# Norm edges between products: one-column sums and wider filler matmuls

## The chip, the core and the metric

The kernel runs on one core of one Trainium2 chip. The metric is device time in microseconds (us). The kernel before takes 2642.19 us, the median of three runs (2640.82 to 2643.86). The engines are named as in the profile: PE is TensorE, PEld its weight loads, DVE is VectorE, ACT is ScalarE, POOL is GpSimd, SP the queue that issues the DMAs. The time is that of the whole program, one launch.

## The reference

Two model blocks in f32, with 512 tokens of width 1024. The first block is a hybrid mixer of four recurrences, cross-attention to a memory, and a convolutional feed-forward network (FFN). The second has two layers whose norms are shifted and scaled by a vector computed from a condition: a layer with a gated recurrence and sparse attention, a layer with a short convolution, each with an FFN. What the change touches is the norm that stands between two matrix products of the second block:

```python
def rms_norm(x, g):
    xf = x.astype(jnp.float32)
    y = xf * lax.rsqrt(jnp.mean(xf * xf, axis=-1, keepdims=True) + EPS)
    return (y * g.astype(jnp.float32)).astype(x.dtype)

def second_block(x, c, ...):
    for i in range(DEPTH_2):
        ...
        h = rms_norm(x, norm_mix_pre[i]) * (1.0 + sc_m) + sh_m
        y = mixer(h, ...)
        x = x + (1.0 + g_m) * rms_norm(y, norm_mix_post[i])
        h = rms_norm(x, norm_ffn_pre[i]) * (1.0 + sc_f) + sh_f
        y = conv_ffn(h, ...)
        x = x + (1.0 + g_f) * rms_norm(y, norm_ffn_post[i])
    return x
```

## The kernel before

All activations lie feature-major: a tile is 128 features by 512 tokens, and 1024 features are KT = 8 tiles. A product multiplies them with weights that stream through a ring of six slots. DVE splits each weight slot into a high and a low part (L324, L326), and PE makes three passes of 128x512 for each pair of tiles (L369, L370, L371); these passes are reduced-precision f32 and one record each in the profile. A plain f32 matmul is two records, with a weight load each.

Between two products stands an edge. Its work is written out by hand, each engine's instructions in program order, with semaphores between the engines; nothing reorders them. The function edge builds four of them (ffn_norm_1, sc_norm, ffn_norm_2 and last_norm), double_edge one (ab_norm). In edge:

- ACT squares the eight output tiles of the product before, POOL adds seven of them. PE adds over the features by matmuls with a constant of ones: L479 for the sum of seven, L482 for the last square, four matmuls each, one for each 128 tokens. The tokens are the stationary operand, the ones the moving one, so every output column holds the same sum.
- ACT takes the root of column 0 (L502), DVE inverts it (L524), PE spreads the four columns over all partitions (spread_root, L471).
- DVE then makes h + y * gain * rstd for eight tiles in turn (L536, L540). For each one ACT squares it (L514) and PE adds it to a second sum (L493, four matmuls). This is the loop of eight turns.
- After the eighth turn root, inverse and spread follow again, and DVE and ACT make the eight tiles that the next product reads (L547, L519, L553). The first of them releases PE's first pass of that product. In last_norm there is no second norm: its PE work ends with the first spread, and the output is stored tile by tile.

Between these steps PE issues matmuls whose result nobody reads, into PSUM bank 1: keep_busy (L662), identity times ones, 128 columns each. There are 11 before the loop, one in each of the first seven turns, and eight behind the second spread.

double_edge joins two norms. Its PE work is L585 (hidden behind the last square), then L588, then L594 and L595 in turns for the second sum, spread_root (L576) for the first norm, three fillers, L576 for the second, eight fillers. Between the spreads stands DVE's inverse L638, which is queued behind the first L620.

Of the kernel before, what the change touches and what calls it, by code (L numbers as in the profile page):

```python
# [24 lines left out]
ALU = mybir.AluOpType  # L25
# [7 lines left out]
P = 128  # L33
# [423 lines left out]
def edge(k, name, before, first_gain, gain=None, shift=None, then=None, y=None):  # L457
# [8 lines left out]
    ones = k.const("ones")  # L466
# [9 lines left out]
    def tensor(pe):  # L476
        pe.wait_ge(added, KT - 1)
        for c in range(TT):
            nc.tensor.matmul(k.psum[:, SUMS + c, 0:P], k.sum_sq[:, c * P:(c + 1) * P], ones, start=True, stop=False)  # L479
        pe.wait_ge(squared, KT)  # L480
        for c in range(TT):
            last = nc.tensor.matmul(k.psum[:, SUMS + c, 0:P], k.squares[:, (KT - 1) % 2, c * P:(c + 1) * P],  # L482
                                    ones, start=False, stop=True)
        last.then_inc(summed, 1)
        spread_root(pe, 0)
        if gain is None:
            return
        pe.wait_ge(out, KT - 2)
        keep_busy(k, pe, 11)
        for j in range(KT):  # L490
            pe.wait_ge(resquared, j + 1)
            for c in range(TT):
                last = nc.tensor.matmul(k.psum[:, SUMS + c, P:2 * P], k.squares[:, j % 2, c * P:(c + 1) * P], ones,  # L493
                                        start=(j == 0), stop=(j == KT - 1))
            last.then_inc(counted, 1)
            if j < KT - 1:
                keep_busy(k, pe, 1)
        spread_root(pe, 1)
        keep_busy(k, pe, 8)

    def root(act, i):
        nc.scalar.activation(k.roots[:, i, :].unsqueeze(2), k.psum[:, SUMS:SUMS + TT, i * P:i * P + 1], ACT.Sqrt,  # L502
                             bias=k.const("eps"), scale=1.0 / D).then_inc(rooted, 1)
# [56 lines left out]
def double_edge(k, name, before, first_gain, gain, shift, then):  # L560
# [10 lines left out]
    ones = k.const("ones")  # L571
# [9 lines left out]
    def tensor(pe):  # L581
        last = (KT - 1) % 2
        pe.wait_ge(added, KT - 1)
        for c in range(TT):
            nc.tensor.matmul(k.psum[:, SUMS + c, 0:P], k.sum_sq[:, c * P:(c + 1) * P], ones, start=True, stop=False)  # L585
        pe.wait_ge(squared, KT)
        for c in range(TT):
            end = nc.tensor.matmul(k.psum[:, SUMS + c, 0:P], k.squares[:, last, c * P:(c + 1) * P], ones,  # L588
                                   start=False, stop=True)
        end.then_inc(summed, 1)  # L590
        pe.wait_ge(added_scaled, KT - 1)
        pe.wait_ge(squared_scaled, KT)
        for c in range(TT):
            nc.tensor.matmul(k.psum[:, SCALED, c * P:(c + 1) * P], k.rstd[:, c * P:(c + 1) * P], ones, start=True, stop=False)  # L594
            end = nc.tensor.matmul(k.psum[:, SCALED, c * P:(c + 1) * P], k.scaled_squares[:, last, c * P:(c + 1) * P], ones,  # L595
                                   start=False, stop=True)
        end.then_inc(summed, 1)
        spread_root(pe, 0)
        keep_busy(k, pe, 3)
        spread_root(pe, 1)  # L600
        keep_busy(k, pe, 8)
# [13 lines left out]
    def vector(dve):  # L615
        link = Link(dve, steps)

        def renew(j):
            if j < KT:
# [11 lines left out]
        nc.vector.tensor_tensor(k.roots[:, 1, :].unsqueeze(2), k.roots[:, 2, :].unsqueeze(2),  # L631
                                k.psum[:, SCALED, :].rearrange("p (c x) -> p c x", x=P)[:, :, 0:1], ALU.mult
# [26 lines left out]
def keep_busy(k, pe, n):  # L659

    for _ in range(n):
        k.nc.tensor.matmul(k.psum[:, 1, 0:P], k.const("ident"), k.const("ones"), start=True, stop=True)  # L662
# [2435 lines left out]
def build(nc, dram, wheres, vec_at):  # L3098

    with ExitStack() as ctx:  # L3100
# [86 lines left out]
        k.roots = k.sb("roots", [P, 4, TT])  # L3187
# [208 lines left out]
```

## Time and profile before

| | before |
|---|---|
| median of three runs | 2642.19 us |
| the profiled execution: its time | 2640.82 us |
| its span (first to last instruction) | 2639.0 us |
| PE busy / PEld busy | 2431.9 / 1974.1 us |
| DVE / ACT / POOL busy | 1751.0 / 666.2 / 207.0 us |
| mean granted clock of PE | 0.956 |
| matmuls of the edges: L493, L662, L471, L482, L479 | 192, 178, 56, 32, 32 records |

PE is busy for 92% of the span. The granted clock is a share of 2.4 GHz; the profile knows two levels, 1.00 and 0.50 (1.2 GHz), and the mean says that PE ran at half clock in some stretches. The views used below: the timeline shows instructions in order of time, merged where the same one repeats; the windows show for a stretch of time how long each engine was busy, how many instructions it had (x) and the granted clock (PEclk). A busy PE is one that has an instruction, which may be one that streams a single column.

### The profile page before, as it was taken

What the parts mean: (1) busy time and instruction counts of PE and PEld (TensorE: products, weight loads), DVE (VectorE), ACT (ScalarE), POOL (GpSimd) and SP (SyncE); (2) the same over time, 40 slices, a digit from 0 to 9 for tenths busy, and PEclk for the clock granted to TensorE, in tenths of its full rate; (3) what the DMA queues carried; (4) which work ended last, traced back from release to release, by engine and by line L of the source; (5) the groups of instructions that cost most, each with busy time, mean ns of one, the idle gap of its engine ahead of it and who ended that gap; (6) DMA issues with size and microseconds to landing.
All of it is one profiled execution on the core that took longest, in us unless ns stands there. A gap on an engine that the chain in (4) does not pass through costs nothing. (4 is left out here: it accounts for less than half of the span.)

```text
span 2639.0 us, 34212 instructions
## 1 busy us (share of the span) xinstructions
PE 2431.9 (92%) x13854; PEld 1974.1 (75%) x13854; DVE 1751.0 (66%) x2724; ACT 666.2 (25%) x1234; POOL 207.0 (8%) x177
## 2 busy tenths in 40 slices
PE   4998877779989999999897979999999999999997
PEld 3885766677678888888674558888888888888886
DVE  6674563774778886525878867766665887766654
ACT  2222332001111120221256760222210211322200
POOL 1001340100100001100013101000001001000000
PEclk9998895889999999999997989999999999999999
DMA  4220001242123335421220007133365353233342
GB/s 150 80 86 2 3 2 49 64 137 71 52 85 96 96 124 199 141 72 64 72 70 18 2 33 262 66 98 99 97 210 183 129 197 130 70 96 96 106 153 68
DMA packets 69324, 252.80 MB, mean 96 GB/s; under 512 B 7696, under 2 KB 7984, under 8 KB 68528
## 3 DMA queue, kind: packets, MB, share of 16 engines
q1 hardware_dynamic: 68592, 248.35, 28.4%
q8 instruction: 110, 1.80, 0.3%
q10 hardware_dynamic: 576, 2.28, 0.2%
q14 instruction: 46, 0.38, 0.0%
HBM read 248.50 MB, written 2.10 MB: 95 GB/s over the span
## 5 line engine op out<-in xcount | busy, mean ns | idle before, releaser
L369 PE MATMUL psum<-rounded_n,rounded_high 128*128 128x512 f32 x1856 | 738.3, 398 | 5.7 <-DVE rounded_n_low L553 2.1
L370 PE MATMUL psum<-rounded_n_low,rounded_high 128*128 128x512 f32 x1856 | 727.9, 392 | 0.0
L371 PE MATMUL psum<-rounded_n,rounded_ring 128*128 128x512 f32 x1856 | 727.2, 392 | 0.0
L326 DVE TENSOR_TENSOR rounded_ring<-ring,rounded_high 128x1024 fp32r<-128x1024 f32 (+1 forms) x360 | 444.5, 1235 | 12.4
L369 PEld LDWEIGHTS psum<-rounded_n,rounded_high 128*128 128x128 f32 x1856 | 352.3, 190 | 87.1 <-issue 11.7
L370 PEld LDWEIGHTS psum<-rounded_n_low,rounded_high 128*128 128x128 f32 x1856 | 352.2, 190 | 76.5 <-issue 4.3
L371 PEld LDWEIGHTS psum<-rounded_n,rounded_ring 128*128 128x128 f32 x1856 | 351.9, 190 | 74.5
L324 DVE CAST rounded_high<-ring 128x1024 fp32r<-128x1024 f32 (+1 forms) x360 | 246.1, 684 | 238.7 <-PE psum L371 223.3
L369 PE MATMUL psum<-rounded_arena,rounded_high 128*128 128x512 f32 x720 | 281.5, 391 | 10.6 <-DVE rounded_ring L326 10.6
L370 PE MATMUL psum<-rounded_arena,rounded_high 128*128 128x512 f32 x720 | 281.1, 390 | 0.0
L371 PE MATMUL psum<-rounded_arena,rounded_ring 128*128 128x512 f32 x720 | 281.1, 390 | 0.0
L2214 DVE SCALAR_TENSOR_TENSOR scratch<-arena,vecs,scratch 128x512 f32<-128x512 f32 x88 | 65.8, 748 | 163.0 <-ACT scratch L2201 163.0
L369 PEld LDWEIGHTS psum<-rounded_arena,rounded_high 128*128 128x128 f32 x720 | 135.8, 189 | 39.1 <-DVE rounded_ring L326 10.9
L371 PEld LDWEIGHTS psum<-rounded_arena,rounded_ring 128*128 128x128 f32 x720 | 135.8, 189 | 28.4
L370 PEld LDWEIGHTS psum<-rounded_arena,rounded_high 128*128 128x128 f32 x720 | 135.9, 189 | 28.2
L2195 ACT COPY arena<-psum 128x512 f32<-128x512 f32 x88 | 51.7, 587 | 351.3 <-PE psum L371 351.3
L2201 ACT ACTIVATE scratch<-arena,vecs 128x512 f32<-128x512 f32 x88 | 63.8, 725 | 199.6 <-DVE arena L2235 198.2
L2288 ACT ACTIVATE scratch<-psum 128x512 f32<-128x512 f32 x32 | 19.2, 600 | 321.9 <-PE psum L371 321.9
L425 POOL TENSOR_TENSOR sum_sq<-sum_sq,scratch 128x512 f32<-128x512 f32 x45 | 68.8, 1530 | 301.8 <-ACT scratch L2288 242.4
L422 POOL COPY sum_sq<-scratch 128x512 f32<-128x512 f32 x7 | 5.1, 725 | 1094.1 <-ACT scratch L2288 838.3
L798 DVE CUSTOM_DVE_ANT_0 arena<-arena 128x1024 f32<-128x1024 f32 x48 | 61.9, 1332 | 14.1 <-DMA arena<-in_mod_w 14.1
L798 DVE CUSTOM_DVE_ANT_0 n_low<-n_low 128x1024 f32<-128x1024 f32 x48 | 56.7, 1220 | 19.6 <-DMA n_low<-in_mod_w 19.6
(466 smaller groups left out, 3050.5 us busy)
## 6 DMA issues: line engine op xcount, KB each, us to landing
ring<-in_w_up SPq DMA_DIRECT2D x132, 512.0 KB, 3.4
ring<-in_w_down SPq DMA_DIRECT2D x48, 512.0 KB, 3.5
n_low<-in_mod_w SPq DMA_DIRECT2D x48, 512.0 KB, 5.2
arena<-in_mod_w SPq DMA_DIRECT2D x48, 512.0 KB, 5.4
ring<-in_w_ab_in SPq DMA_DIRECT2D x37, 512.0 KB, 3.5
ring<-in_w_mix_in SPq DMA_DIRECT2D x31, 512.0 KB, 3.5
ring<-in_w_sc_in SPq DMA_DIRECT2D x24, 512.0 KB, 4.8
ring<-in_w_down SPq DMA_DIRECT2D x24, 384.0 KB, 3.2
```

Source lines behind the costliest of these rows:

```text
L324: nc.vector.tensor_copy(self.rounded(high), raw).then_inc(self.weights_rounded, 1)
L326: nc.vector.tensor_tensor(self.rounded(raw), raw, self.rounded(high), ALU.subtract).then_inc(self.weights_split, 1)
L369: self.nc.tensor.matmul(out, w_high, x_high, start=first, stop=False)
L370: self.nc.tensor.matmul(out, w_high, x_low, start=False, stop=False)
L371: return self.nc.tensor.matmul(out, w_low, x_high, start=False, stop=last)
L422: nc.gpsimd.tensor_copy(total, sq).then_inc(added, 1)
L425: nc.gpsimd.tensor_tensor(total, total, sq, ALU.add).then_inc(added, 1)
L798: k.nc.vector.tensor_tensor_reduce(out=self.tiles[:, i % 3], in0=self.tiles[:, i % 3], in1=self.cond, scale=1.0, scalar=0.0, op0=ALU.mult, ...
L2195: nc.scalar.copy(x, k.psum[:, j % PRODUCT_BANKS, :]).then_inc(out, 1)
L2201: nc.scalar.activation(dst, x, ACT.Copy, scale=taps[:, col:col + 1]).then_inc(tapped, 1)
L2214: link(nc.vector.scalar_tensor_tensor(dst, src[:, 0:T], taps[:, col:col + 1], dst, ALU.mult, ALU.add))
L2288: nc.scalar.activation(k.squares[:, j % 2, :], k.psum[:, j % PRODUCT_BANKS, :], ACT.Square).then_inc(squared, 1)
```

## The change

The sums over features get a moving operand of one column in place of 128, so each writes one column of PSUM, and the readers (L502, L605, L631) are adapted. keep_busy's matmul gets wider, 512 moving columns in place of 128, and is called less often: in edge twice before the loop (11 before) and twice behind it (8 before), in double_edge once and twice (3 and 8 before). Inside the loop stands a filler of 256 columns after each of the eight turns, the eighth included, where there was one of 128 after the first seven. The fillers read the table of vectors instead of ones. The tile of roots has three rows in place of four, since double_edge uses three.

```diff
--- before.py
+++ after.py
@@ -463,7 +463,7 @@
         k.sem(f"{name}_{s}") for s in ("summed", "rooted", "inverted", "spread", "renewed", "resquared", "counted",
                                        "scaled", "shifted", "steps", "done"))
     SUMS, SPREAD = 4, 2
-    ones = k.const("ones")
+    one = k.const("ones")[:, 0:1]
 
     def spread_root(pe, i):
         pe.wait_ge(inverted, i + 1)
@@ -476,30 +476,29 @@
     def tensor(pe):
         pe.wait_ge(added, KT - 1)
         for c in range(TT):
-            nc.tensor.matmul(k.psum[:, SUMS + c, 0:P], k.sum_sq[:, c * P:(c + 1) * P], ones, start=True, stop=False)
+            nc.tensor.matmul(k.psum[:, SUMS + c, 0:1], k.sum_sq[:, c * P:(c + 1) * P], one, start=True, stop=False)
         pe.wait_ge(squared, KT)
         for c in range(TT):
-            last = nc.tensor.matmul(k.psum[:, SUMS + c, 0:P], k.squares[:, (KT - 1) % 2, c * P:(c + 1) * P],
-                                    ones, start=False, stop=True)
+            last = nc.tensor.matmul(k.psum[:, SUMS + c, 0:1], k.squares[:, (KT - 1) % 2, c * P:(c + 1) * P], one,
+                                    start=False, stop=True)
         last.then_inc(summed, 1)
         spread_root(pe, 0)
         if gain is None:
             return
         pe.wait_ge(out, KT - 2)
-        keep_busy(k, pe, 11)
+        keep_busy(k, pe, 2)
         for j in range(KT):
             pe.wait_ge(resquared, j + 1)
             for c in range(TT):
-                last = nc.tensor.matmul(k.psum[:, SUMS + c, P:2 * P], k.squares[:, j % 2, c * P:(c + 1) * P], ones,
+                last = nc.tensor.matmul(k.psum[:, SUMS + c, 1:2], k.squares[:, j % 2, c * P:(c + 1) * P], one,
                                         start=(j == 0), stop=(j == KT - 1))
             last.then_inc(counted, 1)
-            if j < KT - 1:
-                keep_busy(k, pe, 1)
+            nc.tensor.matmul(k.psum[:, 1, 0:T // 2], k.const("ident"), k.vecs[:, 0:T // 2], start=True, stop=True)
         spread_root(pe, 1)
-        keep_busy(k, pe, 8)
+        keep_busy(k, pe, 2)
 
     def root(act, i):
-        nc.scalar.activation(k.roots[:, i, :].unsqueeze(2), k.psum[:, SUMS:SUMS + TT, i * P:i * P + 1], ACT.Sqrt,
+        nc.scalar.activation(k.roots[:, i, :].unsqueeze(2), k.psum[:, SUMS:SUMS + TT, i:i + 1], ACT.Sqrt,
                              bias=k.const("eps"), scale=1.0 / D).then_inc(rooted, 1)
 
     def scalar(act):
@@ -568,7 +567,7 @@
                                        "steps", "done"))
     SUMS, SPREAD, SCALED = 4, 3, 0
     AHEAD = 3
-    ones = k.const("ones")
+    one = k.const("ones")[:, 0:1]
 
     def spread_root(pe, i):
         pe.wait_ge(inverted, i + 1)
@@ -582,23 +581,23 @@
         last = (KT - 1) % 2
         pe.wait_ge(added, KT - 1)
         for c in range(TT):
-            nc.tensor.matmul(k.psum[:, SUMS + c, 0:P], k.sum_sq[:, c * P:(c + 1) * P], ones, start=True, stop=False)
+            nc.tensor.matmul(k.psum[:, SUMS + c, 0:1], k.sum_sq[:, c * P:(c + 1) * P], one, start=True, stop=False)
         pe.wait_ge(squared, KT)
         for c in range(TT):
-            end = nc.tensor.matmul(k.psum[:, SUMS + c, 0:P], k.squares[:, last, c * P:(c + 1) * P], ones,
+            end = nc.tensor.matmul(k.psum[:, SUMS + c, 0:1], k.squares[:, last, c * P:(c + 1) * P], one,
                                    start=False, stop=True)
         end.then_inc(summed, 1)
         pe.wait_ge(added_scaled, KT - 1)
         pe.wait_ge(squared_scaled, KT)
         for c in range(TT):
-            nc.tensor.matmul(k.psum[:, SCALED, c * P:(c + 1) * P], k.rstd[:, c * P:(c + 1) * P], ones, start=True, stop=False)
-            end = nc.tensor.matmul(k.psum[:, SCALED, c * P:(c + 1) * P], k.scaled_squares[:, last, c * P:(c + 1) * P], ones,
+            nc.tensor.matmul(k.psum[:, SCALED, c:c + 1], k.rstd[:, c * P:(c + 1) * P], one, start=True, stop=False)
+            end = nc.tensor.matmul(k.psum[:, SCALED, c:c + 1], k.scaled_squares[:, last, c * P:(c + 1) * P], one,
                                    start=False, stop=True)
         end.then_inc(summed, 1)
         spread_root(pe, 0)
-        keep_busy(k, pe, 3)
+        keep_busy(k, pe, 1)
         spread_root(pe, 1)
-        keep_busy(k, pe, 8)
+        keep_busy(k, pe, 2)
 
     def scalar(act):
         act.wait_ge(summed, 1)
@@ -628,8 +627,7 @@
         dve.wait_ge(summed, 2)
 
         link(nc.vector.tensor_tensor(k.roots[:, 2, :], k.roots[:, 2, :], k.roots[:, 0, :], ALU.mult))
-        nc.vector.tensor_tensor(k.roots[:, 1, :].unsqueeze(2), k.roots[:, 2, :].unsqueeze(2),
-                                k.psum[:, SCALED, :].rearrange("p (c x) -> p c x", x=P)[:, :, 0:1], ALU.mult
+        nc.vector.tensor_tensor(k.roots[:, 1, :], k.roots[:, 2, :], k.psum[:, SCALED, 0:TT], ALU.mult
                                 ).then_inc(scaled, 1)
         dve.wait_ge(spread, 1)
         dve.wait_ge(out, KT)
@@ -659,7 +657,7 @@
 def keep_busy(k, pe, n):
 
     for _ in range(n):
-        k.nc.tensor.matmul(k.psum[:, 1, 0:P], k.const("ident"), k.const("ones"), start=True, stop=True)
+        k.nc.tensor.matmul(k.psum[:, 1, :], k.const("ident"), k.vecs[:, 0:T], start=True, stop=True)
 
 
 def load_inputs(k):
@@ -3184,7 +3182,7 @@
                                              k.vec("ffn_norm")))
         k.tables.pop()
         k.clear_stage_semaphores()
-        k.roots = k.sb("roots", [P, 4, TT])
+        k.roots = k.sb("roots", [P, 3, TT])
         k.arena = k.sb("arena", [P, 50 * T])
         k.rest = k.sb("rest", [P, 476])
         hidden_buffers(k)
```

PE's program at the edge ffn_norm_1, from its first sum into the loop, before (consts is the identity or ones, scratch a square; xN repeats):

```order
L479 MATMUL psum<-consts,sum_sq 128x128 x4
L482 MATMUL psum<-consts,scratch 128x128 x4
L471 MATMUL psum<-consts,roots 128x128 x4
L662 MATMUL psum<-consts 128x128 x11
L493 MATMUL psum<-consts,scratch 128x128 x4
L662 MATMUL psum<-consts 128x128
L493 MATMUL psum<-consts,scratch 128x128 x4
L662 MATMUL psum<-consts 128x128
```

and now (vecs is the table of vectors that the fillers read):

```order
L479 MATMUL psum<-consts,sum_sq 128x1 x4
L482 MATMUL psum<-consts,scratch 128x1 x4
L471 MATMUL psum<-consts,roots 128x128 x4
L660 MATMUL psum<-vecs,consts 128x512 x2
L493 MATMUL psum<-consts,scratch 128x1 x4
L496 MATMUL psum<-vecs,consts 128x256
L493 MATMUL psum<-consts,scratch 128x1 x4
L496 MATMUL psum<-vecs,consts 128x256
```

The order of the steps is the same; the eleven fillers are two wide ones, the sums have one column, and the filler of a turn has 256. The loop's end on PE, before:

```order
L493 MATMUL psum<-consts,scratch 128x128 x4
L662 MATMUL psum<-consts 128x128
L493 MATMUL psum<-consts,scratch 128x128 x4
L471 MATMUL psum<-consts,roots 128x128 x4
L662 MATMUL psum<-consts 128x128 x8
L369 MATMUL psum<-rounded_n,rounded_high 128x512
```

and now:

```order
L493 MATMUL psum<-consts,scratch 128x1 x4
L496 MATMUL psum<-vecs,consts 128x256
L493 MATMUL psum<-consts,scratch 128x1 x4
L496 MATMUL psum<-vecs,consts 128x256
L471 MATMUL psum<-consts,roots 128x128 x4
L660 MATMUL psum<-vecs,consts 128x512 x2
L369 MATMUL psum<-rounded_n,rounded_high 128x512
```

One filler has come between the last sum and the spread. The double edge on PE, from the last pair of the second sum to the last filler, before:

```order
L594 MATMUL psum<-consts,rstd 128x128
L595 MATMUL psum<-consts,scratch 128x128
L576 MATMUL psum<-consts,roots 128x128 x4
L662 MATMUL psum<-consts 128x128 x3
L576 MATMUL psum<-consts,roots 128x128 x4
L662 MATMUL psum<-consts 128x128 x8
```

and now:

```order
L593 MATMUL psum<-consts,rstd 128x1
L594 MATMUL psum<-consts,scratch 128x1
L575 MATMUL psum<-consts,roots 128x128 x4
L660 MATMUL psum<-vecs,consts 128x512
L575 MATMUL psum<-consts,roots 128x128 x4
L660 MATMUL psum<-vecs,consts 128x512 x2
```

Nothing has moved past a spread there; widths and counts alone differ. DVE's, ACT's, POOL's and SP's programs have the same instructions in the same order, with L631 reading four neighbouring columns.

## Rows read from the trace of the kernel before

**Rows 1.** The page, parts 1 and 2: busy time of PE; its granted clock in 40 slices.

```profile
PE 2431.9 (92%) x13854; PEld 1974.1 (75%) x13854; DVE 1751.0 (66%) x2724; ACT 666.2 (25%) x1234; POOL 207.0 (8%) x177
...
PEclk9998895889999999999997989999999999999999
```

**Rows 2.** The page, part 4: the chain that ended last, by line.

```profile
PE psum L369 12%; PE psum L371 12%; PE psum L370 12%; PE psum L493 1%; PE psum L662 0%; PE psum L471 0%; DVE h L540 0%; DVE n L536 0%; PE psum L482 0%; PE psum L479 0%; DVE rounded_n_low L553 0%; DVE n_low L547 0%; ACT rounded_n L519 0%; ACT roots L502 0%; DVE roots L524 0%
```

**Rows 3.** Timeline, edge ffn_norm_1: start, us, engine, line, operation, xcount, [idle before].

```profile
1666.96 0.97 PEld L482 LDWEIGHTS psum<-consts,scratch 128*128 128x128 f32 x8
...
1668.69 0.97 PEld L471 LDWEIGHTS psum<-consts,roots 128*128 128x128 f32 x8 [0.76 <-DVE roots L524]
...
1669.68 2.62 PE L662 MATMUL psum<-consts 128*128 128x128 f32 x22
1669.89 0.75 DVE L536 SCALAR_TENSOR_TENSOR n<-n,mod_cols,psum 128x512 f32<-128x512 f32 x1 [1.25 <-PE psum L471]
...
1672.07 0.97 PEld L493 LDWEIGHTS psum<-consts,scratch 128*128 128x128 f32 x8
...
1673.45 0.97 PEld L493 LDWEIGHTS psum<-consts,scratch 128*128 128x128 f32 x8 [0.19 <-ACT scratch L514]
...
1683.48 1.16 PE L471 MATMUL psum<-consts,roots 128*128 128x128 f32 x8 [0.57 <-DVE roots L524]
...
1687.08 0.19 PEld L369 LDWEIGHTS psum<-rounded_n,rounded_high 128*128 128x128 f32 x1 [0.85 <-issue]
```

**Rows 4.** Timeline, the double edge.

```profile
1097.21 0.39 PE L371 MATMUL psum<-rounded_arena,rounded_ring 128*128 128x512 f32 x1
...
1099.04 0.97 PEld L588 LDWEIGHTS psum<-consts,scratch 128*128 128x128 f32 x8 [0.74 <-ACT scratch L1983]
...
1101.72 0.97 PEld L576 LDWEIGHTS psum<-consts,roots 128*128 128x128 f32 x8
...
1103.59 0.17 DVE L638 RECIPROCAL roots<-roots 128x4 f32<-128x4 f32 x1
```

**Rows 5.** Windows, the loop of ffn_norm_1: stretch, us, busy (x), PEclk, DMA, GB/s.

```profile
1672.10:1683.40 11.30, 10.80 (x80) 9.28 (x79) 8.89 (x14) 4.67 (x8) 0.00 (x0) 1.00 0.01 1
```

**Rows 6.** Windows of L860 alone, then of L662 alone: PE and PEld.

```profile
87.90:90.20 2.30, 2.29 (x22) 2.29 (x21) 1.00 0.50 134
...
1669.80:1672.10 2.30, 2.30 (x22) 2.30 (x21) 1.00 0.01 4
```

**Rows 7.** Matmul durations of L2383 and L493: ns min/median/max.

```profile
L2383 PE MATMUL psum<-vecs,arena x64: 182/250/353, 1160.5 to 1183.1; 128*128 128x1 f32 x64
...
L493 PE MATMUL psum<-consts,scratch x192: 275/275/377, 1672.1 to 2258.0; 128*128 128x128 f32 x192
```

**Rows 8.** Timeline of PE: f32 matmuls with 256 and 512 columns.

```profile
647.28 1.89 PE L2071 MATMUL psum<-mem_k,z_att 128*128 128x256 f32 x8
...
1239.78 1.88 PE L2414 MATMUL psum<-arena 128*128 128x512 f32 x4
```

**Rows 9.** Windows around one run of L2383.

```profile
1179.50:1182.60 3.10, 3.10 (x30) 3.09 (x29) 0.00 (x0) 0.00 (x0) 0.00 (x0) 1.00 0.00 0
1182.80:1189.40 6.60, 6.60 (x18) 5.33 (x18) 0.16 (x1) 0.00 (x0) 0.00 (x0) 0.50 0.00 0
1189.60:1192.00 2.40, 2.40 (x12) 1.97 (x11) 0.00 (x0) 0.03 (x1) 0.00 (x0) 1.00 0.00 0
```

**Rows 10.** Window over L1494 (two columns) at half clock.

```profile
442.10:448.80 6.70, 6.70 (x33) 6.70 (x33) 2.12 (x3) 3.09 (x5) 0.00 (x0) 0.50 0.89 352
```

**Rows 11.** Windows at the end of the projection ab_in.

```profile
1394.00:1397.60 3.60, 1.45 (x7) 0.87 (x5) 3.53 (x4) 2.63 (x6) 0.53 (x1) 1.00 0.27 92
1397.80:1404.00 6.20, 0.00 (x0) 0.00 (x0) 6.13 (x6) 4.53 (x8) 3.77 (x3) 0.50 0.06 22
```

**Rows 12.** Timeline of PE: product matmuls at half clock.

```profile
1184.79 0.63 PE L369 MATMUL psum<-rounded_n,rounded_high 128*128 128x512 f32 x1
1185.21 0.63 PE L370 MATMUL psum<-rounded_n_low,rounded_high 128*128 128x512 f32 x1
```

## The prediction

> **What bounds the kernel now.** I read the page first. TensorE (PE) is busy 2431.9 of 2639.0 us and its granted clock is full in most slices [rows 1], and in the chain of waits the matmuls of the products stand first; of the edges' own lines only L493 reaches 1% [rows 2]. So the kernel is bound by PE nearly everywhere, and where it is not, by short chains between PE, ACT and DVE. The change touches such chains alone: the five edges, that is the norm between two products.
>
> Next, the timeline of one edge, which stands for three (ffn_norm_1, sc_norm and ffn_norm_2 run alike) [rows 3]. When ACT has the product's last square, four sums over 128 columns (L482) start their loads, at 1666.96; four spreads start at 1668.69; DVE gets them at 1669.89. Then comes a loop of eight turns. Its pace is DVE's: the loads of L493 start 1.38 us apart (1672.07, 1673.45) and PE's loads stand only 0.19 us in between. After the eighth turn PE idles 0.57 us for the root and its inverse, runs the spread from 1683.48, and the next product starts at 1687.08. PE waits there for DVE and ACT, so its fillers (L662) are free as long as they end in time. The double edge is shorter: from 1099.04 PE runs 12 sum matmuls in one piece until the spread at 1101.72, and a second spread waits for L638 [rows 4]. In all of this the granted clock is 1.00 [rows 5].
>
> **The change, term by term, with the clock as it is.** In the rows one f32 matmul is two records.
>
> Narrow sums. Is a matmul with one moving column cheaper than one with 128? In one stretch of 2.30 us at full clock 21 loads of L860 (two columns) start; in 2.30 us of L662 (128 columns) also 21 [rows 6]. Both are 0.11 us apart: the load of 128 stationary columns sets the pace, and the change keeps these loads. Only the last record ends sooner, 250 for 275 ns, and the first after a stop takes 182 for 377 ns [rows 7]; since the second record waits for the first, I take 0.1 us for a group of four, bounds 0.03 and 0.2. Eight groups are on a path (four first sums of the edges, three last turns, one in the double edge): -0.8 us. The 16 records of L594 and L595 keep their pace, so the spread at 1101.72 stays.
>
> The Trainium skill ("TensorE: Matmul & The Clock Gate", section "Back-to-back issue gap") gives about 60 cycles for 1 to 64 columns, a floor near 25 ns; by that alone eight records would take 0.2 us instead of 0.9. Its section on LDWEIGHTS gives columns over 1.2 GHz, 107 ns for 128, and with that one the trace agrees (0.11 us).
>
> Fillers. A 128x256 record takes 0.216 us (eight in 1.89, the last 0.38 long) and a 128x512 record 0.43 us (four in 1.88, the last 0.59) [rows 8]. First filler: 22 x 0.112 = 2.46 us becomes 4 x 0.43 = 1.72, ending at 1671.4, before L493's first load at 1672.07; no effect. In a turn, 8 x 0.112 + 0.43 = 1.32 us against DVE's 1.38: it just fits. The new one after the eighth turn, 0.43, lies in the 0.57 us of root and inverse. The last, 1.79 becomes 1.72, lies before 1687.08. Double edge: 0.67 becomes 0.86; from 1101.72 spread (0.89) and filler end at 1103.47, L638's result is there at 1103.77. Four columns fewer in roots and L631's read cost nothing. Sum at full clock: 2640.8 - 0.8 = 2640.0.
>
> **The clock.** What changes more is what PE streams. Before, a turn streams 128 columns in all of its ten records, back to back for 1.12 of 1.38 us. After, wide work is 0.43 us of 1.38, and 0.89 us goes to records that load 128 columns and stream one. What the clock does on such work the trace shows at L2383, also one column wide: in 1179.50 to 1182.60 PE is busy all the time with 30 such records at clock 1.00, and then the clock is 0.50 in 1182.80 to 1189.40, nearly all of it dense product already [rows 9]. L1494, two columns wide, stays at half all through 33 records with PE busy [rows 10]. And a stretch with less than half wide work loses it too: 1394.0 to 1397.6 holds 1.45 us of product, no more, and 0.50 follows [rows 11]. The loop has less wide work than that, 0.43 of 1.38 us against 1.45 of 3.60, and it lasts 11 us. So I expect the clock to fall from 2.4 to 1.2 GHz inside each of the three loops. No row fixes the turn; the dense first filler guards the first of them, and I take the fall after three of the eight.
>
> At half clock a narrow record takes 6.7 us / 33 = 0.21 us [rows 10], and a product's record 0.42 to 0.43 us (1184.79 to 1185.21) [rows 12], both about twice what they take at full clock; the filler's record of 256 columns took 0.216 at full clock and takes, doubled like these, 0.43, its two 0.85. A turn: 8 x 0.213 + 0.85 = 2.56 us. PE, not DVE, then sets the pace: 1.18 us more for each of about five turns, 5.9 us (bounds: two turns, 2.4; seven, 8.3). Behind the loop (all at half clock): filler 0.85 for a wait of 0.57, +0.3; spread 8 x 0.213 for 8 x 0.112, +0.8; last fillers 3.41 us for the 2.7 between the spread's last load and 1687.08, and then product at half clock until it rises, +1.1 together or more. But these are 5 us of dense work, and after 6.6 us of such work the clock was back in rows 9; I take half of this 2.2, 1.1, bounds 0.3 and 4. Less the 0.2 of narrow sums: 5.9 + 1.1 - 0.2 = 6.8 us an edge, 20.4 for three.
>
> Double edge: from the product's end at 1097.6 to 1101.72 PE streams next to nothing, so the clock falls in or just behind it. Full cost if it falls midway: 8 records of sums x 0.1, the spread 0.8, the filler 1.71 for the 1.2 until L638's result, 0.5; 2.1 us. Falling later costs about 0.5. I take 1.3 (bounds -0.1 and 2.7). The last edge has one spread behind its sums: 0.1, at most 0.7. Sum: 2640.8 + 20.4 + 1.3 + 0.1 = 2662.6. The profiled execution, 2640.82 with its span of 2639.0, lies 1.4 below the median 2642.19; half of this added gives 2663.
>
> **Rivals.**
> 1. The clock holds: one wide filler in each turn is enough, and no stop of PE is longer than before by much. For it: PE stays "busy" in nearly all of the loop, and the fillers are there. Then the sum at full clock stands, 2640.0 to 2642: no change. Against: rows 9, busy all the time and fallen. The Trainium skill (same page, section "Why this matters for your kernels") asks only that no long idle gaps part the matmuls; by this rule the clock would hold in the loop, and the time would be this rival's. The trace disagrees at L2383.
> 2. It falls only where hardly anything is streamed (behind the products, 1666.96 to 1668.69 and in the double edge) or in one loop, and the wide fillers bring it back: two or three falls of 1 to 3 us, or one loop of 6.8; 2643 to 2649, say 2646. For it: the first filler is dense for 1.72 us.
> 3. The other side, faster: one-column matmuls cost by their columns after all, since L860 and L2383 read other operands. Then eight groups on a path lose 0.8 us each, and the 16 records of L594 and L595 1.2 more: 2640.8 - 7.6 = 2633. It decides if eight L493 records take under 0.3 us. Against: rows 6, at the same load of 128 columns.
>
> **How the numbers follow.** Forecast (half clock in all three loops) 0.72, own range 2651 to 2672: 3.5 to 10 us for each loop. Rival 1: 0.12. Rival 2: 0.12. Rival 3: 0.04. The range starts at 2644, above rival 1 and taking in most of rival 2, and goes to 2673: it leaves out rivals 1 and 3 and a little of the rest, 0.2 in all. A change of 0.2% (5.3 us) is about what a measurement can tell from none. Slower by more: the forecast and most of rival 2, 0.81. Faster by more: rival 3, 0.04. Same: 0.15.
>
> **What would show it.** Clock 0.50 in stretches inside the loops of L493 and near 1100 us; L493's loads 2.56 us apart in these and 1.38 before the fall; eight loads of L493 in 0.9 us at full clock, not 0.2; the first load of L482 to the next product's first load some 27 us apart where it was 20.1. A granted clock of 1.00 through all loops would make the prediction wrong, and so would narrow records that are less than 0.1 us apart.

## The result and the profile after

The changed kernel takes 2677.8 us (median of 4 runs, 2676.6 to 2681.1), beside it the kernel before 2641.9 (2640.8 to 2643.9): ratio 1.0135, 95% interval 1.0118 to 1.015, slower. The prediction had the sign, but 2663 and the upper end 2673 were too low. The profiled execution, which is not one of these four, took 2672.26 us with a span of 2670.4, so 31.4 us more in the span than before.

The page after, parts 1, 2 and 4: busy time of PE, its clock in 40 slices, the chain by line.

```profile
PE 2467.2 (92%) x13754; PEld 1984.5 (74%) x13754; DVE 1747.2 (65%) x2724; ACT 666.5 (25%) x1234; POOL 210.0 (8%) x177
...
PEclk9998986899999999999897999899999899899999
...
PE psum L369 12%; PE psum L370 12%; PE psum L371 12%; PE psum L493 1%; PE psum L496 1%; PE psum L471 0%; DVE n L535 0%; DVE h L539 0%; PE psum L660 0%; DVE rounded_ring L326 0%; DVE rounded_high L324 0%; DVE rounded_n_low L552 0%; DVE n_low L546 0%; ACT rounded_n L518 0%; ACT scratch L513 0%
```

Against [rows 1, 2], the clock has an 8 in slices 26, 32 and 35 (each 66.8 us wide), the slices of the three edges with a loop, where it had a 9, and L496, the filler in the loop, has entered the chain. (Lines behind the loop's filler stand one or two numbers lower than before: L660 is the filler L662, L513 is L514, L575 is L576, L593 and L594 are L594 and L595.)

The edge ffn_norm_1 in the timeline after, answering [rows 3]: its front, the loads of the loop's turns, and its end.

```profile
1671.71 0.97 PEld L482 LDWEIGHTS psum<-consts,scratch 128*128 128x128 f32 x8
...
1673.33 0.97 PEld L471 LDWEIGHTS psum<-consts,roots 128*128 128x128 f32 x8 [0.65 <-DVE roots L523]
...
1676.71 0.97 PEld L493 LDWEIGHTS psum<-consts,scratch 128*128 128x128 f32 x8 [1.33 <-ACT scratch L513]
...
1678.09 0.97 PEld L493 LDWEIGHTS psum<-consts,scratch 128*128 128x128 f32 x8 [0.19 <-ACT scratch L513]
...
1680.86 0.97 PEld L493 LDWEIGHTS psum<-consts,scratch 128*128 128x128 f32 x8 [0.19 <-ACT scratch L513]
...
1682.27 2.04 PEld L493 LDWEIGHTS psum<-consts,scratch 128*128 128x128 f32 x8
...
1684.50 0.63 ACT L513 ACTIVATE scratch<-h 128x512 f32<-128x512 f32 x1 [0.93 <-PE psum L493]
1684.83 2.04 PEld L493 LDWEIGHTS psum<-consts,scratch 128*128 128x128 f32 x8
...
1692.65 1.91 PEld L471 LDWEIGHTS psum<-consts,roots 128*128 128x128 f32 x8 [0.23 <-DVE roots L523]
...
1697.29 0.19 PEld L369 LDWEIGHTS psum<-rounded_n,rounded_high 128*128 128x128 f32 x1 [1.16 <-issue]
```

Up to the fourth turn the loads are 1.38 us apart, with the wait of 0.19 for ACT between; from the fifth they are 2.56 apart (1682.27, 1684.83), PE no longer waits, and ACT waits for PE. The windows before and behind that point answer [rows 5]:

```profile
1672.10:1681.80 9.70, 8.63 (x57) 6.66 (x57) 8.28 (x13) 3.05 (x7) 0.00 (x0) 1.00 0.16 53
...
1681.90:1695.50 13.60, 13.60 (x53) 12.14 (x52) 4.46 (x8) 2.45 (x5) 0.00 (x0) 0.50 0.01 1
```

PE is "busy" for all of the second stretch, at 1.2 GHz. The edge sc_norm does the same, but ffn_norm_2 doesn't: there the clock falls twice, once just behind the first wide filler's start and again after the loop's third turn.

```profile
2265.60:2268.90 3.30, 3.30 (x6) 1.24 (x5) 3.19 (x5) 1.00 (x2) 0.00 (x0) 0.50 0.01 2
2269.00:2272.30 3.30, 3.30 (x27) 3.20 (x28) 3.20 (x6) 1.42 (x3) 0.00 (x0) 1.00 0.00 0
2272.40:2289.40 17.00, 17.00 (x63) 14.92 (x63) 5.86 (x10) 3.38 (x6) 0.00 (x0) 0.50 0.00 0
```

The other place where time went is one that the change doesn't name: the products that read the arena. The arena is the large tensor whose tiles are the moving operand of 2160 passes (3 x 720 records). Here are its groups at L369 and L370, of before and then of after.

```profile
L369 PE MATMUL psum<-rounded_arena,rounded_high 128*128 128x512 f32 x720 | 281.5, 391 | 10.6 <-DVE rounded_ring L326 10.6
L370 PE MATMUL psum<-rounded_arena,rounded_high 128*128 128x512 f32 x720 | 281.1, 390 | 0.0
```

```profile
L369 PE MATMUL psum<-rounded_arena,rounded_high 128*128 128x512 f32 x720 | 285.2, 396 | 10.6 <-DVE rounded_ring L326 10.6
...
L370 PE MATMUL psum<-rounded_arena,rounded_high 128*128 128x512 f32 x720 | 284.9, 396 | 0.0
```

Durations overlap, so the pace is better read from the number of loads in 100 us. Windows in the last feed-forward block at clock 1.00: the first is inside its second product (reads the arena), the other inside its first (reads n); before, then after.

```profile
2500.00:2600.00 100.00, 100.00 (x443) 82.84 (x442) 52.97 (x64) 10.32 (x17) 8.66 (x6) 1.00 0.43 138
2300.00:2400.00 100.00, 100.00 (x443) 82.84 (x442) 61.92 (x81) 23.75 (x38) 0.00 (x0) 1.00 0.31 96
```

```profile
2540.00:2640.00 100.00, 100.00 (x430) 80.36 (x429) 45.01 (x57) 7.54 (x14) 13.30 (x7) 1.00 0.35 108
2320.00:2420.00 100.00, 100.00 (x443) 82.77 (x442) 63.95 (x85) 22.64 (x37) 0.00 (x0) 1.00 0.31 98
```

With n as moving operand there are 442 loads in both kernels. With the arena there are 429 after: a pass takes 0.233 us instead of 0.226, in a window where PE never stops and the clock is full.

**The 31.4 us by place.** Taking the first load of each product and of each edge as marks, the double edge lasts 14.25 us (before 11.29), the three others 26.66, 26.70 and 28.68 (before 21.19 each) and the last 17.53 (17.64). That is 2.96 + 5.47 + 5.51 + 7.49 - 0.11 = 21.3 us. The stretches of product that read the arena got longer too: 359.97 to 363.50, 358.74 to 362.25 (twice), 173.76 to 175.03 and 89.47 to 90.64, together 13.0. The sum is 34.3; the remaining -2.9 lies in stretches that the change leaves alone (-2.5 of it in the first 737 us). Executions differ by more than that there: the double edge begins between 1093.7 and 1103.5 us in four profiled executions whose program is the same up to there (the kernel before and three of the experiments below).

### The profile page after: what moved, and what is told of

Read it like the earlier page. It is cut to its first block and busy times, and to the rows that moved or that the text cites. A ratio compares the mean times of both kernels' runs of the same rounds, so it can differ in the third digit from the quotient of the medians.

```text
span 2670.4 us, 34012 instructions
## 1 busy us (share of the span) xinstructions
PE 2467.2 (92%) x13754; PEld 1984.5 (74%) x13754; DVE 1747.2 (65%) x2724; ACT 666.5 (25%) x1234; POOL 210.0 (8%) x177
## 5 line engine op out<-in xcount | busy, mean ns | idle before, releaser
L369 PE MATMUL psum<-rounded_n,rounded_high 128*128 128x512 f32 x1856 | 738.8, 398 | 4.1 <-DVE rounded_n_low L650 1.9
L370 PE MATMUL psum<-rounded_n_low,rounded_high 128*128 128x512 f32 x1856 | 728.3, 392 | 0.0
L326 DVE TENSOR_TENSOR rounded_ring<-ring,rounded_high 128x1024 fp32r<-128x1024 f32 (+1 forms) x360 | 442.0, 1228 | 12.4
L369 PEld LDWEIGHTS psum<-rounded_n,rounded_high 128*128 128x128 f32 x1856 | 352.9, 190 | 88.5 <-issue 12.9
L370 PEld LDWEIGHTS psum<-rounded_n_low,rounded_high 128*128 128x128 f32 x1856 | 352.7, 190 | 76.9 <-issue 4.3
L369 PE MATMUL psum<-rounded_arena,rounded_high 128*128 128x512 f32 x720 | 285.2, 396 | 10.6 <-DVE rounded_ring L326 10.6
L370 PE MATMUL psum<-rounded_arena,rounded_high 128*128 128x512 f32 x720 | 284.9, 396 | 0.0
L369 PEld LDWEIGHTS psum<-rounded_arena,rounded_high 128*128 128x128 f32 x720 | 135.3, 188 | 43.8 <-DVE rounded_ring L326 10.9
L370 PEld LDWEIGHTS psum<-rounded_arena,rounded_high 128*128 128x128 f32 x720 | 135.4, 188 | 33.1
L796 DVE CUSTOM_DVE_ANT_0 arena<-arena 128x1024 f32<-128x1024 f32 x48 | 61.9, 1333 | 14.3 <-DMA arena<-in_mod_w 14.3
```

Of the source, the lines that this page charges most:

```text
L326: nc.vector.tensor_tensor(self.rounded(raw), raw, self.rounded(high), ALU.subtract).then_inc(self.weights_split, 1)
L369: self.nc.tensor.matmul(out, w_high, x_high, start=first, stop=False)
L370: self.nc.tensor.matmul(out, w_high, x_low, start=False, stop=False)
L796: k.nc.vector.tensor_tensor_reduce(out=self.tiles[:, i % 3], in0=self.tiles[:, i % 3], in1=self.cond, scale=1.0, scalar=0.0, op0=ALU.mult, ...
```

## The experiments

The theory for the first batch: two causes, the arena's place (13 to 14 us) and the clock lost to the narrow sums in the loops (about 21). Rivals: the arena's products are slow for another reason, a late effect of the edges; and the clock falls for the thinner fillers, not the sums.

**The changed kernel with four rows in roots** (arena back on its line):

```
-        k.roots = k.sb("roots", [P, 3, TT])
+        k.roots = k.sb("roots", [P, 4, TT])
```

> The changed kernel with the roots tile back at four rows, so that the arena starts again at a multiple of 2048 bytes (before: byte 124928; changed kernel: 124960). Theory, place: the product's passes that read the arena took 0.2333 us apart instead of 0.2267 in the changed kernel; 2160 of them x 0.0066 = 14.3 us, which go away: 2677.8 - 14.3 = 2663.5, with these passes again 0.2267 apart and the falls of the clock left as they are. Rival, clock alone: the slower passes are a consequence of the clock's falls, and the roots tile costs nothing: 2677.8 +- 2, passes still 0.2333 apart.

Measured: 2660.6 us (2656.3 to 2673.3, 4 runs), ratio 1.009 [1.0061, 1.012]; 20.0 above the kernel before on the same chip (2640.6); the changed kernel stood 35.9 above the kernel before in its own measurement. One row that nothing reads gives back 16 of these. Its arena groups:

```profile
L369 PE MATMUL psum<-rounded_arena,rounded_high 128*128 128x512 f32 x720 | 281.0, 390 | 11.0 <-DVE rounded_ring L326 11.0
```

The clock still falls in the edges, which last 14.25, 26.80, 24.16 and 27.27 us. The three with a loop cost 14.7 us here where they cost 18.5 in the changed kernel's trace, since the clock falls in other turns. So not all of the 16 us need be the arena's; the passes account for 13.0 in the trace.

**The kernel before with three rows** (the same edit the other way round):

> The kernel before with three rows of roots in place of four, nothing else. Theory, place: 2641.9 + 14.3 = 2656, no fall of the clock in the edges, arena passes 0.2333 us apart. Rival, clock alone: no change, 2642 +- 2.

Measured: 2654.9 us (2651.3 to 2662.4), ratio 1.0056 [1.0037, 1.0076]; 14.3 above the kernel before. The four edges between products stay at 11.3 and 21.2 us, the granted clock never falls in them, and the arena's groups are those of the changed kernel:

```profile
L369 PE MATMUL psum<-rounded_arena,rounded_high 128*128 128x512 f32 x720 | 285.8, 397 | 10.6 <-DVE rounded_ring L326 10.6
```

So the place acts alone, without the other edits, and the two causes add up: 14.3 here and 20.0 for the kernel above make 34.3, beside 35.9 between the medians of the changed kernel and the one before, and 31.4 between their profiled spans.

**The kernel before with the new fillers and its own wide sums** (not shown below: keep_busy's matmul becomes 512 columns wide, the 8 fillers behind the spread 2, and the double edge's 3 and 8 fillers 1 and 2):

```
-        keep_busy(k, pe, 11)
+        keep_busy(k, pe, 2)
...
-            if j < KT - 1:
-                keep_busy(k, pe, 1)
+            nc.tensor.matmul(k.psum[:, 1, 0:T // 2], k.const("ident"), k.vecs[:, 0:T // 2], ...)
```

> The kernel before (128-column sums, four rows of roots) with the changed kernel's fillers (2 of 512 columns, one of 256 in each turn, 2 of 512 behind; 1 and 2 in the double edge). Theory: the narrow sums, not the fewer fillers, let the clock fall: with 128 columns in the sums it stays at 1.00 through all edges, a turn of the loop takes 1.38 us, and the time is that of before, 2642 +- 2. Rival: the thinned fillers are the cause; then clock 0.50 appears in the loops and the time is 2650 or more.

Measured: 2643.3 us (2637.6 to 2647.1, 10 runs), ratio 1.0004 [0.9995, 1.0013], no difference. The window over its edge ffn_norm_1 (1672.17 to 1693.37):

```profile
1672.10:1693.00 20.90, 19.34 (x123) 14.71 (x121) 15.06 (x23) 7.89 (x14) 0.00 (x0) 1.00 0.08 26
```

The clock holds. The new fillers alone cost neither clock nor time, as the forecast had it.

**The kernel before with narrow sums in the loop alone:**

```
-                last = nc.tensor.matmul(k.psum[:, SUMS + c, P:2 * P], k.squares[:, ...], ones,
+                last = nc.tensor.matmul(k.psum[:, SUMS + c, P:P + 1], k.squares[:, ...], ones[:, 0:1],
```

> The kernel before with one edit: in the loop of sixteen turns of the norms between products the four sums write one column instead of 128; the fillers, the sums ahead of the loop and behind it, the double edge and all places of tensors are as before. Theory A, the narrow sums in the loop alone let TensorE's clock fall to half: turns of 2.56 us instead of 1.38 within the loop, an edge of about 26 us instead of 21.19, three of them +14, time about 2656. Theory B, the fall also needs the 256-column fillers: edges stay at 21.2 us, 2641. A fall that starts later or earlier than in the changed kernel tells how much the fillers carry.

(The loop has eight turns, not sixteen.) Measured: 2658.3 us (2656.3 to 2659.4, 3 runs), ratio 1.0075 [1.0052, 1.0098]. The three edges last 25.41, 26.62 and 26.38 us, +14.8. Windows over ffn_norm_1 ahead of the fall and behind it:

```profile
1667.00:1677.50 10.50, 9.93 (x81) 9.17 (x80) 8.95 (x14) 3.75 (x8) 0.00 (x0) 1.00 0.17 52
1677.60:1691.30 13.70, 13.13 (x62) 12.86 (x62) 6.13 (x11) 3.69 (x7) 0.00 (x0) 0.50 0.00 0
```

With the kernel above this closes the case against the sums: the old fillers, the old places, nothing changed but 96 matmuls that are one column wide, and the clock is gone after the loop's fourth turn. PE was busy for 9.93 of 10.50 us ahead of the fall; busy is not enough.

**The changed kernel with four rows and a filler of 384 columns in each turn:**

```
-            nc.tensor.matmul(k.psum[:, 1, 0:T // 2], k.const("ident"), k.vecs[:, 0:T // 2], ...)
+            nc.tensor.matmul(k.psum[:, 1, 0:3 * P], k.const("ident"), k.vecs[:, 0:3 * P], ...)
```

> The changed kernel with four rows of roots and a filler of 384 columns instead of 256 in each turn. Theory, streamed work decides: a turn at full clock takes 8 x 0.112 + 0.64 = 1.54 us, PE-bound, 0.15 us over DVE's 1.38, 24 turns: +3.7 us; wide work is 0.64 of 1.54 us instead of 0.43 of 1.38, so the clock falls later or not at all in the loops: if it holds, some 2642 + 3.7 + 3 (double edge) = 2649. Rival, the narrow records alone decide whatever stands between them: falls as before, a turn at half clock is 1.71 + 1.28 = 2.99 us, and the time is above that with the 256-column filler by 24 x 0.3 or so, 2668 or more.

Measured: 2647.8 us (2643.7 to 2658.1, 10 runs), ratio 1.0035 [1.002, 1.005]. In its profiled execution the clock falls in no loop; it falls ahead of two of them, at 1669.5 and 2051.8 us, and is back within the first turn. A turn is now 1.54 us instead of 1.38, PE setting the pace at full clock, and the edges last 22.98, 22.99 and 22.07 us. So with more wide work in each turn the loops kept the clock in this execution, and an edge cost 0.9 to 1.8 us where it had cost 5.5 to 7.5. The other runs have no trace; three of the ten took 2655 us or more, so falls in them are not ruled out.

**The change at the double edge alone:**

> The kernel before with the change made at the double edge alone (its sums one column wide, its fillers 512 columns); roots stay at four rows. The forecast's step for this edge: half clock behind the sums, +1.3 us on 11.29. What the changed kernel's trace has there: +2.96 us. If the extra belongs to this edge by itself it stays at 14.25 us here and the time is about 2644; if it came with the placement or the other edits it goes to 12.6 and the time to 2642.5. The other edges stay at 21.19 us.

Measured: 2639.7 us (8 runs), ratio 0.9999 [0.9986, 1.0011]. The times show no cost (the interval ends at +2.9 us), but the trace has the 3 us: this edge lasts 14.25 us again. It begins at 1093.7 us here, 3.5 earlier than in the kernel before, and such differences between executions hide it. The changed kernel's windows at this edge and its timeline, answering [rows 4]:

```profile
1099.00:1101.50 2.50, 1.84 (x17) 1.76 (x17) 2.23 (x4) 1.51 (x3) 0.00 (x0) 1.00 0.75 234
1101.60:1108.40 6.80, 6.80 (x27) 5.72 (x27) 2.64 (x8) 0.30 (x1) 0.00 (x0) 0.50 0.94 345
```

```profile
1103.75 1.83 PEld L575 LDWEIGHTS psum<-consts,roots 128*128 128x128 f32 x8
...
1105.67 1.91 PE L660 MATMUL psum<-vecs,consts 128*128 128x512 f32 x2
...
1106.58 0.17 DVE L636 RECIPROCAL roots<-roots 128x4 f32<-128x4 f32 x1
```

The clock falls amid the sums, 10 of the 16 loads of L593 and L594 take twice as long, and the spread begins 3.70 us behind the first load of L587, the last square's sum (1100.05 to 1103.75), where it was 2.68.

**Where the arena must lie.** Three kernels put tensors elsewhere through the gap that `sb` puts in front; nothing else in the kernel before is changed.

```
-        gap = -self.nc.sbuf_base % line if size % line == 0 else 0
+        gap = (at - self.nc.sbuf_base) % line if size % line == 0 else 0
```

> The kernel before with the arena 64 bytes past a line of 2048 bytes (before: on the line; in the changed kernel: 32 bytes past it, where the arena-fed products ran at 0.2333 us a pass instead of 0.2267). Theory A, only an odd multiple of 32 bytes costs: those 2160 passes stay at 0.2267 us, time 2641. Theory B, anything off the 2048-byte line costs: 0.2333 us, 2160 x 0.0066 = +14.3 us, time 2655.

Measured: 2642.1 us (8 runs), ratio 1.0003 [0.999, 1.0016]. Its trace shows a part of the cost all the same: the last feed-forward block takes 359.91 us for 358.74, a third of what the changed kernel loses there, and one of the three groups is slow:

```profile
L369 PE MATMUL psum<-rounded_arena,rounded_high 128*128 128x512 f32 x720 | 284.6, 395 | 10.6 <-DVE rounded_ring L326 10.6
...
L370 PE MATMUL psum<-rounded_arena,rounded_high 128*128 128x512 f32 x720 | 281.0, 390 | 0.0
```

So theory A isn't quite right either.

> The kernel before with the arena 1280 bytes past a line of 2048 (a multiple of 256 bytes). Theory A, only an odd multiple of 32 bytes costs: 0.2267 us a pass, 2641. Theory B, anything off the 2048-byte line costs: 0.2333 us, 2655. If this one stays at 0.2267 us and the one at 64 bytes does not, the line that counts lies between 64 and 256 bytes.

Measured: 2640.1 us (8 runs), ratio 0.9999 [0.9978, 1.002], the groups as before. So being off the 2048-byte line isn't by itself what costs.

The third has the weights' buffers (ring, high) and h, n and n_low 32 bytes off, and the arena on its line:

> The kernel before with the arena on its line, and the weight ring, h, n and their low parts each 32 bytes past a line. Theory A, the moving operand's place alone counts: the products that read n (5568 passes) go from 0.2267 to 0.2333 us, +36.7 us, and those that read the arena (2160 passes, whose weights now lie 32 bytes off) stay at 0.2267 us: time about 2678. Theory B, either operand's place counts: the arena's products slow down too, +51 us, 2693. Theory C, it is something of the arena alone: no product changes, 2641.

Measured: 2653.2 us (3 runs), ratio 1.0055 [1.0032, 1.0077]. None of the three theories: the products that read n, both operands 32 bytes off, are as fast as ever, and those that read the arena, which is on its line, are slow (lines here are one higher than before).

```profile
L372 PE MATMUL psum<-rounded_n,rounded_ring 128*128 128x512 f32 x1856 | 727.8, 392 | 0.0
...
L370 PE MATMUL psum<-rounded_arena,rounded_high 128*128 128x512 f32 x720 | 286.0, 397 | 10.6 <-DVE rounded_ring L327 10.6
...
L370 PE MATMUL psum<-rounded_att_high,rounded_high 128*128 128x512 f32 x64 | 25.4, 397 | 2.4 <-PEq L2127 2.4
```

The third line is the cross-attention's product, whose moving tile is also still on its line: it had 391 ns in the kernel before and is slow here too. Nor is it something behind the arena that moves with it, since here all of that is where it was. So it isn't the moving operand's place alone, but how it lies to the weights' place: the pass is slow where one of the two begins on a line of 2048 bytes and the other 32 bytes past one. The last of these tests it where the two theories differ most, **the changed kernel with all these tensors 32 bytes past their lines**, three rows in roots as the change has them:

> The changed kernel as it is, with every tensor that fills whole lines of 2048 bytes (weights, h, n, the attention's tiles) put 32 bytes past its line, as the arena is in the changed kernel. Theory A, what costs is that the weights and the moving tile lie differently against a 64-byte line: all products run at 0.2267 us a pass, the arena-fed ones too; rounded_arena groups back at 390 ns and the time at 2677.8 - 14.3 = 2663.5. Theory B, a moving tile 32 bytes off is slow whatever the weights do: the arena's groups stay at 396 ns and n's rise to that, 2677.8 and more, up to 2700.

Measured: 2663.1 us (2658.7 to 2666.2, 4 runs), ratio 1.0082 [1.0062, 1.0102]; 21.5 above the kernel before instead of 35.9, with the arena still 32 bytes off. Its window in the last arena product, and its group:

```profile
2530.00:2630.00 100.00, 100.00 (x443) 82.81 (x442) 48.97 (x57) 8.94 (x17) 8.65 (x6) 1.00 0.39 123
```

```profile
L369 PE MATMUL psum<-rounded_arena,rounded_high 128*128 128x512 f32 x720 | 280.9, 390 | 10.6 <-DVE rounded_ring L326 10.6
```

**The opposite edit elsewhere.** If one-column matmuls lose the clock, widening those that the kernel before has should gain. First the 32 at L2383, then also the two-column sums L860 and L1494:

```
-                last = nc.tensor.matmul(k.psum[:, (6, 4)[kind], 0:1], cmp_w1[:, kind, j, :],
-                                        pe_vec[:, j:j + 1], ...)
+                last = nc.tensor.matmul(k.psum[:, (6, 4)[kind], 0:P], cmp_w1[:, kind, j, :],
+                                        pe_vec[:, j:j + 1].broadcast_to([P, P]), ...)
```

> The kernel before with the opposite edit at another place: the 32 matmuls of one column at L2383 (0.112 us apart at full clock, paced by the weight loads) read their column repeated to 128 and write 128 columns. Theory A, one-column matmuls let the clock fall there (two stretches of 6.8 us at half clock at 1162.2 and 1182.7): both stretches go, each gives back about half its length, -6.8 us, time about 2635. Theory B, the clock falls there for the transition itself: nothing changes, 2641, or slower by the wider passes, 2645.

Measured: 2635.9 us (2630.7 to 2644.3, 12 runs), ratio 0.9982 [0.997, 0.9993]. Both falls of the clock at L2383 are gone, and the profiled stretch from the double edge to ffn_norm_1 lasts 550.61 us for 557.38, -6.8 as expected. The second kernel adds this at L860, and the same at L1494:

```
-                        last = nc.tensor.matmul(k.psum[:, 6, 8 * i + 2 * c:8 * i + 2 * c + 2],
-                                                k.ratio[:, i, c * P:(c + 1) * P], pair, start=True, stop=True)
+                        last = nc.tensor.matmul(k.psum[:, 6, 8 * i + 2 * c:8 * i + 2 * c + P],
+                                                k.ratio[:, i, c * P:(c + 1) * P],
+                                                pair.unsqueeze(1).broadcast_to([P, HD, 2]), start=True, stop=True)
```

> The kernel of the wide L2383 with the two-column sums of L860 (32 matmuls) and L1494 (48) widened to 128 columns in the same way. Theory A: the stretch of 6.8 us at half clock at 90.4 us goes as well, -3.4 us more; the half clock at 442 to 448.6, where TensorE also idles, may stay: time about 2632 to 2635. Theory B, wide sums cost more than the clock gives back: L1494's 48 at half clock take 0.427 us instead of 0.19, up to +5 us, time about 2640.

Measured: 2627.5 us (2618.1 to 2634.6, 7 runs), ratio 0.9949 [0.9929, 0.9969]: faster than both kernels of this case, and than either theory had it. The expectation took records for matmuls at these two lines (they are 16 and 32 matmuls), and it was wrong about L1494: its clock came back too. Timeline of PE there, before and then in this kernel.

```profile
440.50 9.01 PE L1494 MATMUL psum<-consts,scratch 128*128 128x2 f32 x48 [1.87 <-ACT scratch L1654]
450.45 7.98 PE L1506 MATMUL psum<-consts,rstd 128*64 128x128 f32 x96 [0.95 <-DVE rstd L1895]
```

```profile
435.15 5.59 PE L1495 MATMUL psum<-consts,scratch 128*128 128x128 f32 x48 [1.87 <-ACT scratch L1655]
441.69 5.46 PE L1507 MATMUL psum<-consts,rstd 128*64 128x128 f32 x96 [0.95 <-DVE rstd L1896]
```

The same 24 matmuls, 48 records, with 64 times the columns take 5.59 us for 9.01, and the spreads behind them 5.46 for 7.98. In the kernel before the clock fell at 442.0 us, 1.5 us into these sums, and in the kernel with the wide L2383 alone at 442.8; here it holds:

```profile
435.00:449.00 14.00, 12.90 (x160) 12.51 (x160) 10.20 (x17) 9.27 (x17) 0.00 (x0) 1.00 0.55 217
```

## Why the prediction was wrong

- **Narrow sums**, 0.1 us for a group: right. Eight records' loads still take 0.97 us, and from L482's first load to the spread's it is 1.62 us (1671.71 to 1673.33) where it was 1.73. Rival 3 is out for matmuls that load 128 columns each. The Trainium skill's 60 cycles for 1 to 64 columns ("TensorE: Matmul & The Clock Gate", "Back-to-back issue gap") are not reached by them either.
- **Fillers** hidden at full clock: right; with wide sums they change nothing (2643.3 against 2640.6, ratio 1.0004).
- **The clock in the loops**, 6.8 us an edge from five slow turns: the fall and the turn at half clock were right (2.56 us forecast and measured; the 0.21 us a record is what the trace has, 0.213, though 6.7 / 33, from which the prediction takes it, is 0.203). The sum, 18.5 us for three against 20.4, is close in part by luck, since two terms missed in opposite directions and the turn in which the clock falls isn't the same each time (14.7 us for three in the trace of the kernel with four rows in roots). In ffn_norm_1 the fall came after the fourth turn instead of the third; three slow intervals cost 3.5 us and not 5.9, while what stands behind was mis-sized the other way: from the eighth turn's load to the spread 2.70 us for 1.73 (that turn's own slowness is in it), and from there to the product 4.64 for 3.6, 2.0 together where the forecast took 1.1 (within its 0.3 to 4). In ffn_norm_2 the fall came after the third turn, as forecast, but also once ahead of the loop, where the dense filler was to guard the clock; that makes it the costliest, 7.49. Rival 1 is disproved by the narrow loop with the old fillers, fallen after 9.93 busy of 10.50 us. The Trainium skill's rule that idle gaps cost the clock (same page, "Why this matters for your kernels") doesn't foresee this fall.
- **The double edge**, 1.3 us: the fall was right, the size was not; 2.96, just above the bound of 2.7. The prediction took the middle between an early and a late fall, and the fall was early. The sums took 1.0 more, the way from the first spread's first load to the second's 1.0 (2.09 to 3.05), and the way from there to the product 1.0 (4.70 to 5.67). In this last part the wide filler holds up the second spread, which the prediction had with 0.5, and that spread begins at half clock, for which it had nothing.
- **The last edge**, 0.1: measured -0.1.
- **"Four columns fewer in roots and L631's read cost nothing"**: this step failed. The read does cost nothing, but the 16 bytes moved the arena, the moving operand of 2160 passes, and cost 13.0 us in the trace, 14.3 alone in the kernel before, and 16 and 14 could be taken back in two ways (four rows; all tensors moved alike). I had looked at the tile as an operand and not at what is allocated behind it; no row of the trace before could have given the price, but the addresses were there to be worked out.

The clock terms alone sum to 21.8 us forecast and 21.3 measured; with the arena's 13.0 the forecast would have been about 2676. What stays open: why a mismatch of 32 bytes costs 0.007 us a pass, why 64 bytes cost a little and 1280 nothing (so what distance counts isn't known beyond the places tried), and the memory products of 256 columns, whose passes with the weights 32 bytes off were 1% faster (294 to 291 ns) and not slower. Nor does any run show what decides the turn in which the clock falls. The last difference, 4 to 5 us between the medians' 35.9 and the 31.4 of the profiled spans, is within the spread of executions.

## What to carry to other kernels

An f32 matmul that loads 128 stationary columns and streams 128 or fewer was paced by that load here (0.11 us a record at full clock), so narrowing its moving side saves next to nothing, and a run of such matmuls can cost TensorE its clock while the profile says busy; widening 80 of them to 128 columns gained 14 us in 2641. Before changing the size of any buffer, work out the addresses of all that is allocated behind it, and compare a group that the change doesn't touch, before and after: its mean duration is the cheapest alarm.

## What the hardware did that I had not expected

- A pass of 128x512 takes 0.226 us where weights and moving tile both start on a line of 2048 bytes or both 32 bytes past one, and 0.233 us where one does and the other doesn't: four placements, six kernels, the same two paces each time (390 and 396 ns in the groups). With the moving tile 64 bytes past its line the groups lie between (395, 390 and 392 ns), with 1280 bytes they are fast.
- The clock fell in the double edge 1.5 us behind L587's first load, with PE fed by one-column matmuls and after one short stop of PE, while in ffn_norm_1's loop it took four turns; no trace of a kernel with wide sums there has a fall at either place.
- At L1494 the clock came back although PE idles 1.87 us ahead of it: the two-column sums, and not the idle time alone, had brought it down.
